# Expert weights fetched in transfers of 2 MB instead of 1 MB, into a ring whose places are filled two at a time

## What is computed

```python
h2 = rms_norm(x, norm_ffn_g)                       # 1024 tokens x 1024
g_logits = h2 @ w_rg + b_rg                        # 4 groups, the top one is taken
top_p, top_e = top_k(softmax(e_in), 2)             # of its 8 experts, the top 2
gate = p_grp * top_p / sum(top_p)
# tokens are sorted by expert and padded to blocks of 128 slots
gu = xi @ w_up[e]                                  # 1024 x 1024 for each of 32 experts
y  = (silu(g) * u) @ w_down[e]                     # 512 x 1024
out = x + scatter_add(y * gate)
```

## Time and profile before

| | us |
|---|---|
| median of 3 runs | 1724.2 (1717.82 to 1725.96) |
| profiled execution, its time | 1726.69 |
| its span in the trace | 1724.8 |
| PE busy | 1655.4 (96%) |
| DVE busy | 1278.8 (74%) |
| ACT busy | 885.3 (51%) |

### The profile page before, as it was taken

The page is one execution under the profiler, slowest core; times in us unless marked ns, Lnnn a source line. Parts: engine busy times, 40 slices in busy tenths (PEclk is TensorE's granted clock), DMA queues, the critical chain, the costliest instruction groups (busy, mean ns, idle before and its releaser), DMA issues.

```text
span 1724.8 us, 25237 instructions
## 1 busy us (share of the span) xinstructions
PE 1655.4 (96%) x8623; PEld 1392.7 (81%) x8623; DVE 1278.8 (74%) x1687; ACT 885.3 (51%) x1131; POOL 361.5 (21%) x293
## 2 busy tenths in 40 slices
PE   6999999999999999999999999699999999999996
PEld 6988887887888878899987788578888888887775
DVE  4034887799999908867658853488989898888885
ACT  5225651211111115768751112477888887777774
POOL 2211122332222210101000000173322222222221
PEclk9999999999999999999999999899999999999998
DMA  5325334432222427466508645599999999999983
GB/s 186 118 106 154 110 118 152 149 101 97 97 95 94 133 89 173 87 141 141 127 26 278 197 154 205 188 330 376 376 377 375 378 376 371 366 359 364 370 318 99
DMA packets 85344, 360.13 MB, mean 209 GB/s; under 512 B 18339, under 2 KB 23459, under 8 KB 60688
## 3 DMA queue, kind: packets, MB, share of 16 engines
q1 hardware_dynamic: 71764, 337.80, 56.1%
q0 software_dynamic: 13504, 21.28, 4.9%
HBM read 314.98 MB, written 61.86 MB: 218 GB/s over the span
## 4 chain that ended last, share of the span: by engine, by line
PE 36%; DMA 16%; DVE 4%; issue 2%; ACT 2%; POOL 1%; SPq 0%; ACTq 0%; DVEq 0%; POOLq 0%
DMA ex_raw<-in_w_expert 14%; PE at_ops L1725 5%; PE at_sps L1688 3%; PE at_tps L1700 3%; PE ex_gp L2536 1%; PE ex_gp L2538 1%; PE ex_gp L2537 1%; PE ex_upp L2536 1%; PE ex_upp L2538 1%; PE ex_upp L2537 1%; PE ex_yp L2538 1%; PE ex_yp L2537 1%; PE ex_yp L2536 1%; PE at_sps L103 1%; PE at_sps L105 1%
## 5 line engine op out<-in xcount | busy, mean ns | idle before, releaser
L1874 DVE TENSOR_TENSOR ex_wl<-ex_raw,ex_wh 128x2048 fp32r<-128x2048 f32 x191 | 433.9, 2288 | 70.1 <-ACT ex_wh L1870 68.5
L1870 ACT ACTIVATE ex_wh<-ex_raw 128x2048 fp32r<-128x2048 f32 x191 | 365.4, 1916 | 98.6 <-DMA ex_raw<-in_w_expert 56.8
L103 PE MATMUL gs_banks<-hT_hi,gs_wh 128*128 128x512 f32 x512 | 199.8, 390 | 1.2 <-PEq L67 1.2
L105 PE MATMUL gs_banks<-hT_hi,gs_wl 128*128 128x512 f32 x512 | 199.2, 389 | 0.0
L104 PE MATMUL gs_banks<-hT_lo,gs_wh 128*128 128x512 f32 x512 | 199.2, 389 | 0.0
L867 ACT ACTIVATE gs_wh<-gs_raw 128x1024 fp32r<-128x1024 f32 x30 | 31.8, 1061 | 254.5 <-PE gs_banks L105 254.4
L929 DVE MATCH_REPLACE8 selm<-sg_top,selm 128x896 f32<-128x896 f32 (+5 forms) x164 | 142.7, 880 | 0.0
L925 DVE MAX8 sg_top<-selm 128x8 f32<-128x896 f32 (+5 forms) x164 | 137.8, 884 | 0.0
L1725 PE MATMUL at_ops<-at_v,at_pT 128*128 128x65 f32 (+1 forms) x984 | 125.0, 269 | 0.0
L812 POOL TENSOR_TENSOR gs_wl<-gs_raw,gs_wh 128x1024 fp32r<-128x1024 f32 x30 | 72.5, 2416 | 237.9 <-ACT gs_wh L867 237.9
L1725 PEld LDWEIGHTS at_ops<-at_v,at_pT 128*128 128x128 f32 x984 | 120.1, 192 | 0.9
(11 more groups left out here) (368 smaller groups left out, 3654.7 us busy)
## 6 DMA issues: line engine op xcount, KB each, us to landing
ex_raw<-in_w_expert SPq DMA_DIRECT2D x192, 1024.0 KB, 26.6
gs_raw<-in_w_gate SPq DMA_DIRECT2D x32, 512.0 KB, 3.6
gatesT<-sg_go SPq DMA_DIRECT2D x32, 512.0 KB, 2.6
selm<-gatesT SPq DMA_DIRECT2D x32, 512.0 KB, 4.4
at_qk<-qkh SPq DMA_DIRECT2D x52, 256.0 KB
at_qk<-qkl SPq DMA_DIRECT2D x44, 256.0 KB
gs_raw<-in_w_qk SPq DMA_DIRECT2D x16, 512.0 KB, 4.9
qkh<-gs_out_hi SPq DMA_DIRECT2D x16, 512.0 KB, 2.6
```

Of the source, the lines that this page charges most:

```text
L103: pe.matmul(out, a_hi, b_hi, start=(k == 0), stop=False)
L105: last = pe.matmul(out, a_lo, b_hi, start=False, stop=(k == len(lhs) - 1))
L1870: act.activation(ring.wh[r][:, :, :], ring.raw[slot][:, :, :], ACT.Copy).then_inc(ring.w_high, 1)
L1874: dve.tensor_tensor(ring.wl[r][:, :, :], ring.raw[slot][:, :, :], ring.wh[r][:, :, :].bitcast(F32), ALU.subtract).then_inc(ring.w_low, 1)
```

## The change

Two neighbouring pairs become one transfer: four weight rows, 16 KB for each partition, 2 MB, three for an expert. The host lays the expert weights out accordingly. The ring keeps its 12 MB and its splits of 1 MB; a transfer fills two neighbouring places, and one semaphore stands for both. SP waits until the second of the two places is free; ScalarE waits for the whole transfer before it splits either half. In the stage of eight tiles the transfers are issued after tiles 1 and 3. The two down pairs of the last block stay transfers of 1 MB each, the second with a semaphore of its own.

```diff
--- before.py
+++ after.py
@@ -1353,12 +1353,11 @@
                     load_x(tile + 2)
                 sp.dma_start(tiles(out)[tile], x2[s][:, :]).then_inc(x2_stored[s], 16)
                 if tile == LAST:
-                    for j in range(UP_PAIRS, PAIRS):
-                        load_pair(sp, a, ring, PAIRS + j, 0, j)
+                    load_quad(sp, a, ring, PAIRS + UP_PAIRS, 0, UP_PAIRS // 2)
                 sp.wait_ge(h2_made, tile + 1)
                 sp.dma_start(tiles(h2d)[tile], h2[s][:, :]).then_inc(h2_stored[s], 16)
-                if 1 <= tile <= len(IN_ROUTE):
-                    load_pair(sp, a, ring, IN_ROUTE[tile - 1], 0, tile - 1)
+                if tile in (1, 3):
+                    load_quad(sp, a, ring, IN_ROUTE[tile - 1], 0, tile // 2)
 
         @block.gpsimd
         def _(pool):
@@ -1841,9 +1840,12 @@
 
         size = PAIR * D * 4
         self.raw_at = {g: base + n * size for n, g in enumerate(self.ORDER)}
-        self.raw = [nc.alloc_sbuf_tensor_at(f"ex_raw{g}", [P, PAIR, D], F32, offset=self.raw_at[g]) for g in range(RAW)]
+        assert all(self.raw_at[g + 1] == self.raw_at[g] + size for g in range(0, RAW, 2))
+        self.quads = [nc.alloc_sbuf_tensor_at(f"ex_raw{q}", [P, 2 * PAIR, D], F32, offset=self.raw_at[2 * q]) for q in range(RAW // 2)]
+        self.raw = [self.quads[g // 2][:, g % 2 * PAIR:(g % 2 + 1) * PAIR, :] for g in range(RAW)]
         self.base, self.end = base, base + RAW * size
-        self.w_loaded = [sem(f"ex_w_loaded{g}") for g in range(RAW)]
+        self.w_loaded = [sem(f"ex_w_loaded{q}") for q in range(RAW // 2)]
+        self.last_loaded = sem("ex_last_loaded")
         self.w_high = sem("ex_w_high")
         self.w_low = sem("ex_w_low")
         self.used = sem("ex_used")
@@ -1860,10 +1862,12 @@
 IN_ROUTE = (2, 3, 4, 5)
 
 
-def load_pair(sp, a, ring, slot, e, j):
+def load_quad(sp, a, ring, slot, e, q, half=None):
     view = a["w_expert"]
     src = view[e] if isinstance(e, int) else view[bass.ds(e, 1)].rearrange("a j p f -> (a j) p f")
-    sp.dma_start(ring.raw[slot][:, :, :].rearrange("p k f -> p (k f)"), src[j]).then_inc(ring.w_loaded[slot], 16)
+    rows = slice(0, 2 * PAIR) if half is None else slice(half * PAIR, (half + 1) * PAIR)
+    sp.dma_start(ring.quads[slot // 2][:, rows, :].rearrange("p k f -> p (k f)"),
+                 src[q][:, rows.start * D:rows.stop * D]).then_inc(ring.last_loaded if half == 1 else ring.w_loaded[slot // 2], 16)
 
 
 def split_high(act, ring, slot, r):
@@ -2012,8 +2016,8 @@
             for stored in landed:
                 for s in range(2):
                     sp.wait_ge(stored[s], 16 * NT // 2)
-            for j in range(UP_PAIRS):
-                load_pair(sp, a, ring, place(0, j), 1, j)
+            for j in range(0, UP_PAIRS, 2):
+                load_quad(sp, a, ring, place(0, j), 1, j // 2)
             sp.wait_ge(planned, 1)
             sp.wait_ge(gathered[0], 16)
             n = trips(sp)
@@ -2021,11 +2025,11 @@
 
             def step(b, s):
                 e = expert(b + 1)
-                for j in range(PAIRS):
+                for j in range(0, PAIRS, 2):
                     if j == UP_PAIRS:
                         e = expert(b)
-                    sp.wait_ge(w_low, position(b, j) - RAW + 1)
-                    load_pair(sp, a, ring, place(s, j), e, j)
+                    sp.wait_ge(w_low, position(b, j + 1) - RAW + 1)
+                    load_quad(sp, a, ring, place(s, j), e, j // 2)
 
             with sp.Fori(0, n) as it:
                 step(it * 2 + 1, 1)
@@ -2033,7 +2037,7 @@
             e = expert(n * 2 + 1)
             for j in range(UP_PAIRS, PAIRS):
                 sp.wait_ge(w_low, position(n * 2 + 1, j) - RAW + 1)
-                load_pair(sp, a, ring, place(1, j), e, j)
+                load_quad(sp, a, ring, place(1, j), e, j // 2, j % 2)
 
         @block.vector
         def _(dve):
@@ -2250,7 +2254,6 @@
                 const(pool.iota(entry[:, q, :, 0], pattern=[[P, NT]], base=0, channel_multiplier=1))
             pool.dma_start(slots.rearrange("(p n) a -> p n a", p=P), empty[:, :, :]).then_inc(emptied, 16)
             pool.sem_inc(ring.w_loaded[0], 16)
-            pool.sem_inc(ring.w_loaded[1], 16)
             for tile in xg:
                 pool.memset(tile[:, :], 0.0).then_inc(cleared, 1)
             rows = dict(bounds_check=T - 1, oob_is_err=False)
@@ -2349,7 +2352,7 @@
             act.preload_act_table_set("natural_log_exp_and_others")
 
             def high_in_route(p):
-                act.wait_ge(ring.w_loaded[p], 16)
+                act.wait_ge(ring.w_loaded[p // 2], 16)
                 split_high(act, ring, p, p % RING)
 
             act.wait_ge(d, marks["group"])
@@ -2379,7 +2382,7 @@
 
             def high(b, s, j, loads):
 
-                act.wait_ge(w_loaded[place(s, j)], loads)
+                act.wait_ge(w_loaded[place(s, j) // 2], loads)
                 act.wait_ge(used, position(b, j) - RING + 1)
                 split_high(act, ring, place(s, j), place(s, j) % RING)
 
@@ -2444,7 +2447,10 @@
             high(n * 2, 0, 4, loads(n, 0))
             high(n * 2, 0, 5, loads(n, 0))
             def last_wait(j):
-                act.wait_ge(w_loaded[place(1, j)], loads(n, 1))
+                if j == UP_PAIRS:
+                    act.wait_ge(w_loaded[place(1, j) // 2], loads(n, 1))
+                else:
+                    act.wait_ge(ring.last_loaded, 16)
                 act.wait_ge(used, position(n * 2, j - 1))
 
             last_wait(UP_PAIRS)
@@ -2640,9 +2646,9 @@
     w_r = np.concatenate([np.asarray(inputs["w_router_group"])[0], np.asarray(inputs["w_router_expert"])[0],
                           zeros(P - GROUPS - EXPERTS)], 1)
     b_r = np.concatenate([np.asarray(inputs["b_router_group"])[0], np.asarray(inputs["b_router_expert"])[0]])
-    in_pairs = lambda m, n: np.asarray(m)[0].reshape(EXPERTS, n, PAIR, P, D).transpose(0, 1, 3, 2, 4)
-    w_expert = np.concatenate([in_pairs(inputs["w_expert_up"], UP_PAIRS), in_pairs(inputs["w_expert_down"], DOWN_PAIRS)],
-                              1).reshape(EXPERTS, PAIRS, P, PAIR * D)
+    in_quads = lambda m, n: np.asarray(m)[0].reshape(EXPERTS, n // 2, 2 * PAIR, P, D).transpose(0, 1, 3, 2, 4)
+    w_expert = np.concatenate([in_quads(inputs["w_expert_up"], UP_PAIRS), in_quads(inputs["w_expert_down"], DOWN_PAIRS)],
+                              1).reshape(EXPERTS, PAIRS // 2, P, 2 * PAIR * D)
     arrays = {
         "x": np.asarray(inputs["x"]).reshape(NT, P, D),
         "norm_mix_g": np.asarray(inputs["norm_mix_g"]).reshape(1, D),
```

## The result

| | before | after |
|---|---|---|
| median of 6 runs | 1724.9 us | 1737.7 us |
| lowest to highest | 1717.8 to 1728.4 | 1734.6 to 1739.6 |
| profiled execution, its span | 1726.7, 1724.8 | 1739.6, 1737.8 |
| ratio to before, 95% interval | | 1.0079 [1.0066, 1.0093] |

The change makes the kernel slower by 0.8%, some 13 us. I had forecast 1722.5 us, and 1735 us as the upper end of the range: both missed.

What follows compares the result with a forecast made beforehand. DMA service of the weights, 37.5 us a ring turn, was taken as the limit, TensorE 12.3 us behind. Terms -5 + 2.4 + 1 = -1.6 us gave 1722.5 us from 1724.2; range 1713 to 1735, 8 times in 10.

Steps and rivals of the forecast that it cites:

- Packets, "I take 5 us of gain": Weight transfers: 16 KB as one packet saves 14 ns per two old ones; 5 us gain, 9 us at most.
- The sign that I had named for this step: SP's queue: packet count falls by about 12,000 and DMA busy share per megabyte by 1 to 2%.
- Gathers beside larger packets: zero: POOL's gathers and scatters: a gather lands 2.4 us later, the loop's first 3 to 3.5 us; net cost zero.
- TensorE had 12.3 us to spare against the transfers, which takes this up whole: Loop's start: TensorE's 12.3 us of slack against later transfers absorbs the first gather's delay; without that cover, 3.5 us cost.
- Filled two at a time: Ring: first of two places stays empty 2.95 us longer, possibly idling DMA engines at the start; cost 1 us, 0 to 3.
- First half waits for second: ScalarE starts a pair only when the next has landed; near the end costs 2.4 us, between 0 and 3.1.
- POOL's slack: POOL's late scatters: 2.4 us longer landing comes out of idle waits for ScalarE, 5.72 and 3.73 us; cost zero.
- The sign by which I would have called the prediction wrong: Between 1450 and 1650: mean DMA busy share well below 0.97, or TensorE never waiting there.
- Cheaper packets with TensorE as the limit: Rival: large packet saving makes transfers never late, TensorE limits; 8.8 us gain, 1715.4 us; chance 17%.
- Doing nothing: Rival: 16 KB are cut into two packets again, the 5 us gain is gone; 1727.6 us; chance 22%.
- The slower rival: Rival: a transfer's 33.4 us way is latency; each ring turn 2.95 us longer, 20 us for seven, 1744; chance 11%.
- The 2 us beside the bytes of each transfer: Skill's rule, cited for the TensorE-limit rival: each transfer costs about 2 us beside its bytes, so merging two saves 2 us.

Runs made afterwards that it cites:

- m2: Load-only kernel, weights alone, 96 transfers of 2 MB into six places, in 16 KB packets instead of 8 KB: 490.5 us.
- m1: Load-only kernel, nothing multiplied: weights alone, 96 transfers of 2 MB into six places, in 8 KB packets: 497.3 us.
- m3: m1 plus a scatter and a gather of 64 rows on partitions 0 to 63 after every third transfer, 8 KB packets: 592.2 us.
- m4: m3 with 16 KB packets instead of 8 KB: 592.7 us.
- m7: m3 with two lists of 1 KB after each gather and five transfers ahead instead of six, 8 KB packets: 594.0 us.
- m8: m7 with 16 KB packets instead of 8 KB: 602.9 us.
- e8: Kernel before with its 1 MB weight transfers in 4 KB packets, one for each weight row: 1737.57 us, 1.0080 of before.
- e7: Changed kernel with neighbouring slots' rows spread alternately over lower and upper 64 partitions: 1722.71 us, 0.9993 of before.
- e10: Changed kernel measured once more, unchanged, on the chip of e9: 1738.34 us, 1.0063 of before.
- e1: Changed kernel with each 2 MB transfer made of 8 KB packets again: 1732.93 us, 1.0039 of before.
- e2: Kernel before, with SP issuing its 1 MB transfers in twos, once both places are free: 1733.72 us, 1.0038 of before.
- e3: Kernel before, with ScalarE starting the first of two pairs only when the second has landed too: 1729.59 us, 1.0011 of before.
- e5: Kernel before with the changed memory layout only: 8 KB packets, neighbouring partitions' reads 16 KB apart: 1723.63 us, 1.0001 of before.
- e9: Kernel before with the rules of e2 and e3 together, transfers still 1 MB in 8 KB packets: 1735.35 us, 1.0046 of before.
- e6: Kernel before with neighbouring slots of every block alternately on lower and upper 64 partitions, spreading the rows: 1718.10 us, 0.9973 of before.

## Why the prediction was wrong

**Packets, "I take 5 us of gain": the wrong sign, and the step that failed.** The count fell as forecast (13,680, against some 12,000) and the gain of the packet itself exists: m2 beats m1 by 1.4%. But the engines of this stage also carry rows and lists, and there it is gone (m3, m4) or reversed (m7, m8). In the kernel it is a loss of 0.2 to 0.4%, 3 to 7 us where I had 5 us of gain. The sign that I had named for this step says the same: the busy share per megabyte should have fallen by 1 to 2%, and from 1500 to 1600 it rose by 1.6% (85.2% for 32.88 MB below, 87.1% for 34.16 in the earlier trace rows). I priced a packet from stretches without row traffic and used the price where there was some.

**"Gathers beside larger packets: zero", with 3 to 3.5 us covered: the delay was priced well, the cover was wrong.** In after's profiled execution each of three small transfers in series (the slots, the list 6.76, the gather 10.65) is 0.7 to 0.8 us longer, and with the 0.6 us from before the loop TensorE starts 2.96 us later (1190.81 against 1187.85). That is the size forecast, for the sum by some luck: the slots and the 0.6 us were not in it, and POOL's own instruction for the gather was 1.55 us shorter. POOL's timelines of before and after:

```profile
1177.88 2.60 POOL L2264 DMA_INDIRECT ex_xg<-h2d,ex_ids_x  x1 [6.28 <-DMA ex_ids_x<-slots]
...
1180.12 1.05 POOL L2267 DMA_INDIRECT ex_xg<-h2d,ex_ids_x  x1 [7.04 <-DMA ex_ids_x<-slots]
```

Without that instruction the first gather takes 6.7 us beside 4 KB packets (e8), 7.1 to 8.4 beside 8 KB (before and seven experiments) and 9.6 to 9.8 beside 16 KB (after, e7, e10): 2.3 us between before and after, against the 2.4 of the estimate. This is the packet's delay with the least else in it. Later gathers take 16.9 us in the window from 1500, against 12.2 and 12.5 in e1, twice the estimate. Dma view of after, 1500 to 1600:

```profile
q1 hardware_dynamic: 2257, 32.88, 85.2%
ex_xg<-h2d,ex_ids_x POOLq DMA_INDIRECT x6, 16.9
ex_ids_o<-slots POOLq DMA_DIRECT2D x5, 1.0 KB, 7.8
```

By the Trainium skill, "DMA: Bandwidth & Descriptors", section "Queues, rings and completion order", each engine takes turns packet by packet, and this trace agrees: 4.7 us more for a gather.

Two things were missing from the step. First, the wait of 3.7 us was followed by 6 us at a clock of 0.50: from 1190.81 the transposes take 1.97 us instead of 1.09, matmuls start 0.43 us apart instead of 0.23, and TensorE's delay grows from 2.96 to 5.8 us (the next transposes at 1211.56, in before at 1205.79). The kernel before waited 1.3 us, and kept 2.4 GHz. Second, "TensorE had 12.3 us to spare against the transfers, which takes this up whole" treats the transfers as if they went on while TensorE stands. They go on only as far as there are free places. In this kernel a place is free only after its weights are split, and the splits wait for TensorE, so a stall of TensorE early in the loop, where the queue is short, becomes idle DMA engines some 10 us later: share 0.60 and 132 GB/s from 1202 to 1206, and in the 50 us from 1200 29 GB/s less than before, 1.45 MB, nearly 4 us of service. Transfers, the later limit, lose their lead as TensorE does. That this very loss makes up the part of the lag not due to longer turns is worked out, not measured apart. e1 shows that it isn't the whole: without such a start it too is 4.9 us behind at split 96.

**Filled two at a time, "+1 us, 0 to 3": the right place, too small.** e2 measures 6.6 us [4.3, 9.0], beyond the 3 us that I had as its most. I had named the idle DMA engines at the start, and given them 1 us. The price was the largest single one, and only a part of its origin can be seen: counted from the packet records in the 120 us around the split from which the lags are formed, SP's queue moves 39.7 MB in before and 39.3 to 39.9 in e3, e5 and e8, but 38.3, 38.6 and 39.1 in e2, e9 and e1, which fill by two; one MB is some 2.7 us of service. In after it is 37.8 and in e10 36.8. The rest stays open, for most of e2's ratio is not found in its one profiled execution (span 1726.6, 1.8 us over before's).

**First half waits for second, "+2.4 us": right.** e3 gives 1.9 us [0, 4.0], and the trace of after shows the very wait: 2.87 us before the pair at 1700.80, then the next without one; the same two splits of before start at 1687.43 and 1690.25. ACT's timeline of after:

```profile
1693.72 1.92 ACT L1874 ACTIVATE ex_wh<-ex_raw 128x2048 fp32r<-128x2048 f32 x1 [0.37 <-DMA ex_raw<-in_w_expert]
1700.80 1.92 ACT L1874 ACTIVATE ex_wh<-ex_raw 128x2048 fp32r<-128x2048 f32 x1 [2.87 <-DMA ex_raw<-in_w_expert]
```

**POOL's slack, right.** In the same block, the last but two, the scatter's landing is waited for longer, 8.21 us where the earlier trace rows had 6.50, and the wait for ScalarE shrinks from 5.72 to 5.02. The last scatter but one, with 3.73 us in the earlier trace rows, has 5.10. POOL's timeline of after:

```profile
1681.86 0.55 POOL L2262 DMA_DIRECT2D ex_ids_o<-slots  x1 [8.21 <-DMA out_x<-ex_xa,ex_ids_o]
1687.43 1.95 POOL L2275 DMA_INDIRECT out_x<-ex_xa,ex_ids_o  x1 [5.02 <-ACT ex_xa L2416]
...
1719.47 1.60 POOL L2275 DMA_INDIRECT out_x<-ex_xa,ex_ids_o  x1 [5.10 <-ACT ex_xa L2416]
```

**The sum.** -5 + 2.4 + 1 + 0 = -1.6 us was forecast for 13 measured. By the runs it reads +1.9 (both) + 6.6 (by two) + 3 to 7 (packet) = 11.5 to 15.5 us. Two terms make the miss: the packet, off by 8 to 12 us with the sign, and the filling by two, off by 5.6. The cost of filling stood near its lower end and that of the gathers at it, the gain in its middle, and the clock had no term at all. The sign by which I would have called the prediction wrong, a DMA share well below 0.97 from 1450 to 1650, did not show either (0.96 to 0.98): the miss lay elsewhere.

**The rivals.** Cheaper packets with TensorE as the limit: the limit exists where I put it, 12.3 us away (e6 is 12.1 us ahead at split 180), but packets don't lead there; levelling the rows does. Doing nothing: refuted by the packet count. The slower rival, a way that is pure latency and 2.95 us more for each turn, is not what happened either: turns grew by 0.65 us, e1 with the same two rules has none of it, and the way fell from 33.4 to 11.1 us in e6 at a higher rate, so it is a queue. My chance of 11% for slower was too low even so, as no case in it was a late gather. The 2 us beside the bytes of each transfer stand in the Trainium skill, "DMA: Bandwidth & Descriptors", in section "Anatomy of one DMA — SWDGE (gpsimd) path", as a fit to transfers issued from GpSimd, not in "Bandwidth" as the prediction says. On SP's queue with several under way they find no support: e1 and e9, 2 MB against 1 MB, are equal.

## What to carry to other kernels

Where small, awaited transfers share the DMA engines with bulk, the size of the bulk packets sets how long the small ones take; 8 KB was best here, and both 4 and 16 KB lost. A stall is covered by another limit's slack only if the other resource keeps working through it: with a ring whose places come free by use it need not, as the 132 GB/s some 10 us after the stall show. Where transfers of fewer partitions than 128 run beside full ones, look at which engines carry them before tuning anything else: spreading the rows of this kernel was worth 0.27%, where none of the change's edits gained.

## What the runs showed of the hardware that I had not expected

- The mean busy share of the DMA engines is 1.02 where 8% less is moved than at 1.01 (387 GB/s in m3 against 422 in m1).
- 64 rows of 4 KB on partitions 0 to 63, gathered and scattered, cost 3.0 us a block (m1 to m3); by the estimate from 159 and 327 ns a packet it would be 1.9 us over all engines.
- 16 KB packets are 1.4% faster alone (m2 to m1) and 1.5% slower with rows, lists and five ahead (m8 to m7).
- TensorE's waits of 2.4 us (e2), 3.7 (after, e7) and 7.0 (e10) were followed by some us with matmuls 0.43 us apart, at 1.2 GHz as the granted clock of 0.50 there says; those of 1.3 (before) and 1.8 us (e9) were not.
- Reads 16 KB apart instead of 8 KB made no difference (1.0001).
